# Six instead of four outputs in the first projection group of each feed-forward part

## The reference

```
def conv_ffn(h, w_gate, w_up, conv_w, conv_b, w_down):       # f0, f1
    a = causal_dwconv(h @ w_gate, conv_w, conv_b)
    return (jax.nn.silu(a) * (h @ w_up)) @ w_down
...
def swiglu(h, w_gate, w_up, w_down):                         # a0, a1, b0, b1
    return (jax.nn.silu(h @ w_gate) * (h @ w_up)) @ w_down
...
def sandwich(x, fn, pre_g, post_g, shift, scale, gate, res_w):
    hn = rmsnorm(x, pre_g) * (1 + scale[:, None, :]) + shift[:, None, :]
    y = rmsnorm(fn(hn), post_g)
    return x + res_w * gate[:, None, :] * y
```

## Time and profile before

| | |
|---|---|
| median of 3 runs | 3756.47 us (3754.92 to 3760.41) |
| the profiled execution's own time | 3753.44 us |
| its span, first to last instruction | 3751.6 us |
| PE busy | 3599.6 us, 96% of the span, 16712 matmuls |
| DVE busy | 2019.4 us, 54% |
| ACT busy | 1332.3 us, 36% |
| POOL busy | 128.5 us, 3% |
| mean granted TensorE clock | 0.978 of full speed |
| data moved | 429.09 MB, 114 GB/s on average |

### The profile page before, as it was taken

How to read it: one execution, slowest core, us unless ns; L and a number is a source line. 1 busy time by engine, 2 the same in 40 slices (tenths; PEclk the granted TensorE clock), 3 DMA queues, 4 the chain that set the end, 5 groups by cost and what they waited for, 6 DMA issues and landing times.

```text
span 3751.6 us, 41675 instructions
## 1 busy us (share of the span) xinstructions
PE 3599.6 (96%) x16712; PEld 2888.0 (77%) x16712; DVE 2019.4 (54%) x3608; ACT 1332.3 (36%) x2291; POOL 128.5 (3%) x126
## 2 busy tenths in 40 slices
PE   6899999999999999998999999999999999989998
PEld 5647888766888888885677888888878888868886
DVE  7856756576757654576765235523553333344233
ACT  3563323353423332234443223323324334333222
POOL 3330000000000000001100000000000000000000
PEclk9989999999999999999999999999999999989999
DMA  6314555422555455521012222222222222212231
GB/s 258 107 40 144 197 193 174 141 80 74 180 194 194 151 190 195 192 101 65 29 51 96 96 96 96 85 96 97 95 83 82 75 83 78 62 55 95 96 101 62
DMA packets 155469, 429.09 MB, mean 114 GB/s; under 512 B 45468, under 2 KB 50524, under 8 KB 155277
## 3 DMA queue, kind: packets, MB, share of 16 engines
q1 hardware_dynamic: 155276, 426.45, 33.5%
HBM read 423.98 MB, written 2.40 MB: 114 GB/s over the span
## 4 chain that ended last, share of the span: by engine, by line
PE 85%; DVE 11%; ACT 2%; issue 1%; DMA 0%; POOL 0%; SPq 0%; ACTq 0%; DVEq 0%; POOLq 0%
PE ps L420 25%; PE ps L421 24%; PE ps L422 24%; PE ps L731 1%; PE ps L457 1%; PE ps L711 1%; PE ps L771 1%; PE ps L809 1%; DVE X L1621 1%; DVE mraw L1456 1%; PE ps L796 1%; DVE HL L1520 1%; PE ps L577 1%; DVE TT L1535 1%; PE ps L470 1%
## 5 line engine op out<-in xcount | busy, mean ns | idle before, releaser
L420 PE MATMUL ps<-HH,whi 128*128 128x512 f32 x3168 | 1254.9, 396 | 26.1 <-DVE HL L1520 13.0
L421 PE MATMUL ps<-HL,whi 128*128 128x512 f32 x3168 | 1238.1, 391 | 0.0
L422 PE MATMUL ps<-HH,wlo 128*128 128x512 f32 x3168 | 1238.0, 391 | 0.0
L1468 DVE TENSOR_TENSOR wlo<-wraw,whi 128x1024 fp32r<-128x1024 f32 x526 | 644.1, 1225 | 774.2 <-ACT whi L934 774.0
L934 ACT ACTIVATE whi<-wraw 128x1024 fp32r<-128x1024 f32 x548 | 576.1, 1054 | 693.5 <-PE ps L422 684.6
L420 PEld LDWEIGHTS ps<-HH,whi 128*128 128x128 f32 x3168 | 597.8, 189 | 166.2 <-issue 35.8
L421 PEld LDWEIGHTS ps<-HL,whi 128*128 128x128 f32 x3168 | 597.9, 189 | 126.1 <-issue 4.9
L422 PEld LDWEIGHTS ps<-HH,wlo 128*128 128x128 f32 x3168 | 597.7, 189 | 126.2
L1456 DVE CUSTOM_DVE_ANT_0 mraw<-mraw,CB 128x1024 f32<-128x1024 f32 x224 | 282.3, 1262 | 0.9 <-DMA mraw<-mst 0.9
L1654 DVE TENSOR_TENSOR TT<-TT,ps 128x512 f32<-128x512 f32 x116 | 79.7, 687 | 212.9 <-PE ps L422 182.2
L420 PE MATMUL ps<-PHf,whi 128*128 128x512 f32 x352 | 136.9, 389 | 0.0
(11 more groups left out here) (327 smaller groups left out, 3928.4 us busy)
## 6 DMA issues: line engine op xcount, KB each, us to landing
wraw<-wst SPq DMA_DIRECT2D x548, 512.0 KB, 3.3
mraw<-mst SPq DMA_DIRECT2D x224, 512.0 KB, 4.3
MR<-mst SPq DMA_DIRECT2D x16, 512.0 KB, 13.8
X<-xt SPq DMA_DIRECT2D x8, 256.0 KB, 5.1
BB<-bvec SPq DMA_DIRECT2D x8, 256.0 KB, 3.4
TT<-lse SPq DMA_DIRECT2D x16, 128.0 KB, 3.0
out<-X SPq DMA_DIRECT2D x8, 256.0 KB, 2.0
CB<-crow SPq DMA_DIRECT2D x2, 512.0 KB, 4.6
```

The source lines that it names most:

```text
L420: e.matmul(o[key], wh, sh(k), start=k == 0, stop=False)
L421: e.matmul(o[key], wh, sl(k), start=False, stop=False)
L422: ins = e.matmul(o[key], wl, sh(k), start=False, stop=k == nk - 1)
L1468: e.tensor_tensor(wlo[:, x % RAW, :], wraw[:, x % RAW, :], whi[:, x % SPLIT, :].bitcast(F32), ALU.subtract).then_inc(*wlo_made.up(x))
```

## The change

The first group of every feed-forward part takes gate and up of column tiles 0, 1 and 2, six outputs, and the pairs begin with tile 3. The plan of the weight stream, PE's program, and the programs of ACT and DVE are changed alike. On ACT and DVE `feed(8)`, product 0, product 1, `feed(16)`, product 2 becomes `feed(24)`, product 0, product 1, product 2; everything after product 2 is in the order of before. The number of matmuls, weight tiles, blocks and products is the same.

```
@@ ffn_groups
-            gs.append((8, [(tag + "g", 0), (tag + "u", 0), (tag + "g", 1), (tag + "u", 1)]))
-            at = 2
+            gs.append((8, [(tag + part, n) for n in range(3) for part in "gu"]))
+            at = 3
@@ tensor_engine, ffn
-                        proj([("g", tag, 0), ("u", tag, 0), ("g", tag, 1), ("u", tag, 1)], 8, hh, hl, normed(s))
-                        i = 2
+                        proj([(part, tag, n) for n in range(3) for part in "gu"], 8, hh, hl, normed(s))
+                        i = 3
@@ scalar_engine, ffn, and the same lines in vector_engine, ffn
-                        feed(8)
-                        product(tag, 0, conv)
-                        product(tag, 1, conv)
-                        i = 2
+                        feed(24)
+                        for i in range(3):
+                            product(tag, i, conv)
+                        i = 3
```

## The result

| | before | six outputs |
|---|---|---|
| median | 3754.92 us (3751.27 to 3762.38, 7 runs) | 3747.04 us (3741.54 to 3752.04, 7 runs) |
| ratio to before | | 0.9973, 95% interval 0.9960 to 0.9985 |
| span of the profiled execution | 3751.6 us | 3745.3 us |

The changed kernel is faster by 0.27% by the ratio, and the interval excludes no change; the medians themselves lie 7.9 us apart, 0.21%. A second measurement of the same two kernels, six_again, gave 3745.39 against 3757.51, 12.1 us apart, ratio 0.9968 (0.9956 to 0.9979); 9.3 us had been expected for it.

What follows compares the result with a forecast made beforehand. PE was taken to bound the kernel, busy 96% of the span, with DVE setting the pace in three first groups. Removing 9.4 us of waits and their effects from the 3756.47 us median gave 3747 us, range 3742 to 3755.

Steps and rivals of the forecast that it cites:

- 13.0 us in 16 waits: PE's waits for HL, the low part of the normed input, read as the only entry this change can reach.
- Pace: First groups: PE asks for a tile every 2.72 us with four outputs, 4.08 with six; DVE makes one in 2.70, plus blocks.
- Six is enough: In a1, the worst, DVE has every HL tile in time; smallest margin 1.6 us at tile 1, 7.0 at the end.
- The sum: First groups save 5.00 us in a1, 2.19 in b0, 2.22 in b1, together 9.41; f0, f1, a0 give 0.
- The clock: a1's half-speed stretch, some 1.5 us of its gain, was read as a consequence of the waits and goes with them.
- the clock keeps its share: Rival: waits go but the half-speed stretch falls elsewhere on dense matmuls; gain 7.9 us, 3748.6 us; chance 0.13.
- ACT and DVE: Three products in a row delay the tenth block in f0 and f1; slack 3.7 to 4.3 us, so cost 0.
- slower rival: Row of three products starves PE of weights at the tenth block of f0 and f1; far row 3778 us; chance 0.03.
- Banks and SP: Banks free with over 10 us of cover, SP's loads six blocks, 32.6 us, ahead of use; both cost 0.
- taken back behind: Rival: half-speed stretches in the norms and mixers behind take the gain back; two more cost 3.0 us, 3750.1 us; chance 0.22.

Runs made afterwards that it cites:

- five: Changed kernel with first groups of five outputs (gate 0, up 0, gate 1, up 1, gate 2), then up 2 alone: 3745.90 us, 0.9971 of before.
- pairs: Kernel before with first groups of two outputs, a pair like all others, and product 0 before the block of weights: 3804.23 us, ratio 1.0125.
- six_early: Six outputs only in f0, f1 and a0, four as before in a1, b0 and b1: 3754.91 us, 0.9995 of the kernel before.
- slow_products: Changed kernel with products 0, 1 and 2 of f0 and f1 lengthened by five repeats of the ACT copy: 3762.35 us, 1.0012 of before.
- six_late: Six outputs only in a1, b0 and b1, four as before in f0, f1 and a0: 3747.58 us, 0.9977 of the kernel before.
- four_mod_early: Kernel before, four outputs everywhere, with DVE's last three mod_steps three blocks of free positions earlier: 3755.48 us, ratio 1.0000.

## Why the prediction was right

The forecast of 3747 us met a median of 3747.04; that it is so close is luck, since medians of the same kernel came out at 3745.4 and 3747.0, and the one before at 3754.9 to 3758.1. Two deviations cancelled: the kernel before came out 1.5 us under the median that the forecast started from, and the medians lie 7.9 us apart where 9.4 were expected. What is right is the mechanism and its size in the three parts. One reading ahead of the steps is too wide: of the 13.0 us in 16 waits that the change was said to reach, only six waits with 5.9 us lay inside a first group of a feed-forward part. The sum does not use the 13.0. The steps:

1. *Pace.* Right. five, pairs and six_early show it from three sides.

2. *Six is enough.* Right. DVE's rows in a1 of the changed kernel, tiles 1, 6 and 7:

```profile
1980.72 0.74 DVE L1520 SCALAR_TENSOR_TENSOR HL<-TT,MOD,HH 128x512 fp32r<-128x512 f32 x1
...
1997.67 0.74 DVE L1520 SCALAR_TENSOR_TENSOR HL<-TT,MOD,HH 128x512 fp32r<-128x512 f32 x1
1999.86 0.75 DVE L1520 SCALAR_TENSOR_TENSOR HL<-TT,MOD,HH 128x512 fp32r<-128x512 f32 x1 [0.80 <-ACT HH L977]
```

PE starts at 1978.90, so tile 1 is ready 2.6 us after that, as in the earlier trace rows (1975.76 - 1973.19), tile 6 at 19.5 and tile 7 at 21.7. DVE's pace did not change when PE's did.

3. *The sum.* Right: 5.00, 2.19 and 2.22 were expected for the three parts, 4.95, 2.14 and 2.18 came. f0, f1 and a0 gave -0.07. The 9 matmuls read from the earlier trace rows as starting at half speed were matmuls in work; 8 start there, so the stretch costs 7 x 0.2267 = 1.6 us, which is what six_early shows without it.

4. *The clock.* Too simple. I called the half-speed stretch a consequence of the wait. It is one that comes in some executions: 1.6 us in two of three profiles. So the gain to expect on average is nearer 9.2 - 1.6 / 3, or 8.7, than 9.4 (an estimate, from three profiles), too small a difference to matter here. The rule of the Trainium skill (TensorE: Matmul & The Clock Gate, "HAM oscillation — how this bites in real kernels"), which puts the fall down to long idle gaps, does not hold alone: a wait of 1.96 us had one behind it twice. The rival built on it, *the clock keeps its share*, has no profile for its first half, that the stretch would stay in the groups: in all six first groups of the changed kernel the clock is 1.00. That it falls elsewhere is taken up with the rivals below.

5. *ACT and DVE.* Right to 0.1 us. Product 0 and the tenth block in f0 of the changed kernel, on ACT and then on DVE:

```profile
376.34 0.78 ACT L1004 ACTIVATE TT<-ps,V 128x512 f32<-128x512 f32 x1 [0.92 <-PE ps L422]
...
389.81 2.00 ACT L934 ACTIVATE whi<-wraw 128x1024 fp32r<-128x1024 f32 x2
```

```profile
390.89 1.23 DVE L1468 TENSOR_TENSOR wlo<-wraw,whi 128x1024 fp32r<-128x1024 f32 x1 [0.26 <-ACT whi L934]
```

The group starts at 346.78. The block is ready at 392.12 and wanted 49.06 us after the start, at 395.8: 3.7 us of slack, the lower of my two values, since DVE was still at a `mod_step` when product 0 came. slow_products measured the same 3.7 as 9.8 - 6.1. The slower rival thus had its place right and its price: only the products were not that slow.

6, 7. *Banks and SP.* No wait for either appears in the changed trace. How wide a group the banks allow was not tried.

Of the rivals, "taken back behind" is half real: the profiled pair lost 2.9 of 9.2 us that way. Most of this looks like scatter. From f0 to f1, the profiles of kernels with four outputs in a1 have 228.25 to 232.33 us and those with five or six 227.7 to 232.35, and the medians of six_again and six_late lie 12.1 and 8.9 us under before. The norm between a1 and b0 is another matter. It takes 13.28 us above, and in the second profile of the kernel before:

```profile
2342.69:2355.99 13.30, 12.45 (x85) 10.72 (x83) 9.47 (x31) 2.17 (x6) 0.00 (x0) 0.87 0.11 39
```

With five or six outputs in a1 it takes 14.66 to 15.06 us in eight profiles of nine; the ninth, slow_products, has 13.29. In four_mod_early and six_early, which have four outputs and no half-speed stretch in a1's group, it takes 14.66. So some 1.4 to 1.8 us of a1's 4.95 were given back right behind it in nearly every profile, at a lower granted clock (0.77 against 0.87). No experiment separates this from chance.

## What to carry to other kernels

Where one engine makes an operand tile by tile and PE uses it as it comes, compare the two times for a tile, from the rows, and count into that engine's time whatever else it does between the tiles (here blocks of weights and a `mod_step`, which made 2.7 us a tile into 3.1). Open as many accumulators as make PE's the longer: here five, and six gained nothing more. Then follow what a wider group eats faster (here blocks of weights and who makes their low parts), as the start of the program shows: the wait had been 11 us for one engine and became 7 us for another. Read such a change by the stretches it touches; the total carries several us from half-speed stretches elsewhere.

## What was not expected of the hardware

A wait of 2 us on TensorE, between dense matmuls, can be followed by 3.4 us at the 1.2 GHz level and need not be: 8 matmuls start in 3.40 us in one profile, 15 in another, behind the same wait. In pairs, with waits of 1.0 to 3.3 us inside the groups, each of the six first groups has one. With waits of 6.1 us it came both times, for 6.8 us from shortly before their end, and made them cost 8.9.
